# Weight scratch in row layout, six-deep halo rows and kept halo pieces in a hybrid decoder layer

## The reference

```
h2 = rmsnorm(x, g_ffn)
a = relu(h2 @ w_ff1)          # 1024 x 4096
x = x + (a * a) @ w_ff2       # 4096 x 1024
return rmsnorm(x, g_final)
```

## Time and profile before

| | us |
|---|---|
| median of 3 runs | 1951.0 (1950.24 to 1951.74) |
| the profiled execution: its time | 1958.57 |
| its span (slowest core, 0) | 1956.5 |
| spans of the other cores | 1927.8 to 1946.8 |
| PE busy | 1636.5 |
| DVE, ACT busy | 992.8, 756.4 |

### The profile page before, as it was taken

How to read it: one execution, slowest core, us unless ns; L and a number is a source line. 1 busy time by engine, 2 the same in 40 slices (tenths; PEclk the granted TensorE clock), 3 DMA queues, 4 the chain that set the end, 5 groups by cost and what they waited for, 6 DMA issues and landing times.

```text
span 1956.5 us, 30675 instructions; the slowest of 8 cores (1927.8 to 1956.5 us)
## 1 busy us (share of the span) xinstructions
PE 1636.5 (84%) x10130; PEld 864.0 (44%) x10320; DVE 992.8 (51%) x1613; ACT 756.4 (39%) x1481; POOL 66.4 (3%) x114
## 2 busy tenths in 40 slices
PE   2655526889959998899889997999799979998798
PEld 1322215445524553455435543555355524553343
DVE  2333226556536654575546645565456535654434
ACT  2222028235522554255414551355334532544212
POOL 4000000000000000000000000000100000000000
PEclk9867768999979998999989998999899999999899
DMA  9999998234254334442454326333542354324243
GB/s 201 159 148 138 183 165 157 89 123 162 87 195 155 120 129 166 164 143 107 145 188 147 130 109 204 135 141 123 200 157 98 133 180 141 125 89 187 103 157 123
DMA packets 72632, 283.85 MB, mean 145 GB/s; under 512 B 7712, under 2 KB 30496, under 8 KB 49824
## 3 DMA queue, kind: packets, MB, share of 16 engines
q1 hardware_dynamic: 37440, 211.00, 31.3%
q0 software_dynamic: 35040, 70.88, 18.6%
HBM read 287.53 MB, written 39.85 MB: 167 GB/s over the span
## 4 chain that ended last, share of the span: by engine, by line
PE 67%; DMA 15%; DVE 7%; issue 4%; ACT 4%; SPq 2%; DVEq 0%; POOL 0%; ACTq 0%; another core or an unknown queue 0%; POOLq 0%
PE mm L406 32%; PE mm L808 19%; DMA xa<-xh 5%; PE ob L646 5%; PE sc L618 5%; DMA out<-x 5%; PE mm L751 4%; DMA ring<-wscratch 2%; DMA x<-xh 2%; ACT tmp L364 2%; SPq L115 2%; PE tp L387 1%; DVE x L814 1%; DVE hb L377 1%; DVE QA L510 1%
## 5 line engine op out<-in xcount | busy, mean ns | idle before, releaser
L406 PE MATMUL mm<-h2T,ring 128*128 128x512 bf16 x2053 | 500.3, 386 | 33.1 <-DVE KT L521 17.8
L808 PE MATMUL mm<-ring,aT 128*128 128x512 bf16 x1977 | 479.7, 387 | 5.7 <-DVE aT L796 1.2
L620 ACT ACTIVATE P<-sc 128x512 bf16<-128x512 f32 x487 | 283.5, 595 | 220.8 <-PE sc L618 195.8
L406 PEld LDWEIGHTS mm<-h2T,ring 128*128 128x128 bf16 x2128 | 202.7, 99 | 247.4 <-issue 49.2
L808 PEld LDWEIGHTS mm<-ring,aT 128*128 128x128 bf16 x2048 | 196.0, 99 | 217.9 <-issue 31.0
L796 DVE TENSOR_TENSOR aT<-tmp 128x512 bf16<-128x512 f32 x256 | 177.1, 692 | 205.6 <-ACT tmp L795 204.3
L795 ACT ACTIVATE tmp<-mm 128x512 f32<-128x512 f32 x256 | 152.8, 597 | 323.8 <-PE mm L406 312.9
L814 DVE TENSOR_TENSOR x<-x,mm 128x512 f32<-128x512 f32 x256 | 175.5, 685 | 142.1 <-PE mm L808 135.0
L406 PE MATMUL mm<-hT,ring 128*128 128x512 bf16 x809 | 194.5, 392 | 43.9 <-DMA ring<-wscratch 24.9
L629 DVE TENSOR_TENSOR P<-P,E 128x512 bf16<-128x512 bf16 x448 | 185.7, 421 | 71.9 <-ACT P L620 69.7
L646 PE MATMUL ob<-P,Vd 128*128 128x128 bf16 x1792 | 176.2, 222 | 49.7 <-DVE P L629 49.5
(11 more groups left out here) (75 smaller groups left out, 1187.7 us busy)
## 6 DMA issues: line engine op xcount, KB each, us to landing
ring<-wscratch SPq DMA_DIRECT2D x176, 1024.0 KB, 5.4
wscratch<-w_ff POOLq DMA_DIRECT2D x16, 1024.0 KB, 230.8
out<-x POOLq DMA_DIRECT2D x32, 512.0 KB, 3.8
xa<-xh SPq DMA_DIRECT2D x24, 512.0 KB, 12.4
xa<-xh POOLq DMA_DIRECT2D x24, 512.0 KB, 5.3
x<-xh POOLq DMA_DIRECT2D x24, 512.0 KB, 5.6
Vd<-Vd SPq DMA_DIRECT2D x132, 48.0 KB, 2.3
wscratch<-w_in POOLq DMA_DIRECT2D x4, 1024.0 KB, 84.2
```

Of the source, the lines that this page charges most:

```text
L406: T.op("pe", lambda: nc.tensor.matmul(out_ap, lhsT=l, rhs=r, start=(i == 0), stop=(i == n - 1)), reads=reads, writes=[b_out], mark=(i == n ...
L620: T.op("act", lambda: nc.scalar.activation(out=P_[:], in_=s_, func=AF.Exp, bias=bt.get("bias", 0.0)), reads=[bs_], writes=[bP_])
L808: T.op("pe", lambda: nc.tensor.matmul(m_[:], lhsT=aT[:, fl, tc * 128:(tc + 1) * 128], rhs=pf[:, fl % 4, ch * 512:(ch + 1) * 512], start=(f ...
```

## The change

It has five parts. (1) The scratch keeps the weights' own row layout in four tensors. The conversions are 8: `w_in` whole (rows of 2048), `w_out` and the quarters of `w_ff2` flat (4096 elements at a time), `w_ff1` in halves (2048). A ring load of `w_in`, `w_out` or `w_ff1` is then 1024 runs of 512 bf16; one of `w_ff2` is 128 runs of 8 KB, four consecutive rows to a partition, which `ff1` answers by taking every fourth column of its piece as weights. (2) Row blocks for the halo tiles, the memory tokens and tile 4 are requested six deep, in the two `xa` and four of the `x1` buffers; gains that are first needed later are loaded after stage B of tile 4. (3) Only pieces 1 and 2 are loaded directly; `w_in` is converted next, ahead of the memory weights, and piece 3 is loaded from the scratch when tile 2 starts. (4) The three halo pieces stay in the ring for tile 4, which takes them in the order 3, 1, 2, 0; `ring_skip(3)` sets the ring's requests three pieces ahead of their use for the rest of the program. (5) Five PSUM banks serve projections up to tile 4's stage B, stage A of the next tile is spread over the groups of stage B, and the memory phase moves behind tile 2.

```diff
-    sc = nc.dram_tensor("wscratch", [NPIECES, 128, 4096], BF16).ap()
+    s_in = nc.dram_tensor("s_in", [D, 2048], BF16).ap()
+    s_out = nc.dram_tensor("s_out", [D, D], BF16).ap()
+    s_ff1 = nc.dram_tensor("s_ff1", [D, 4096], BF16).ap()
+    s_ff2 = nc.dram_tensor("s_ff2", [4096, D], BF16).ap()
...
+        def ring_src(idx):
+            if idx >= P_FF2:
+                i = idx - P_FF2
+                return s_ff2[512 * i:512 * i + 512, :].rearrange("(p f) c -> p (f c)", f=4), b_cv[f"ff2_{i // 2}"], 1
+            if idx >= P_FF1:
+                i = idx - P_FF1
+                return s_ff1[:, 512 * i:512 * i + 512].rearrange("(k p) c -> p k c", p=128), b_cv[f"ff1_{i // 4}"], 8
...
+        xpool = [(xa[i], b_xa[i], xa_sem[i]) for i in range(2)] + [(x1[i], b_x1[i], x1_sem[i]) for i in range(1, NX1)]
+        halo_rows = [xh[c * 128:(c + 1) * 128, :] for c in range(4 * NHALO)]
+        halo_rows += [memd[c * 128:(c + 1) * 128, :] for c in range(2)]
+        halo_rows += [xh[c * 128:(c + 1) * 128, :] for c in range(4 * NHALO, 4 * NHALO + 4)]
...
+        halo_issue()
+        T.dma("sp", g_sem, gb_mix[:], gbs[0])
+        halo_issue()
+        T.dma("sp", g_sem, csm_t[:], csm[:, :])
         T.dma("sp", g_sem, cpc_t[:], cpc[:, :, :])
...
+        for _ in range(4):
+            halo_issue()
+        T.dma("sp", gm_sem, x1[0][:], gbs[3], writes=[b_x1[0]])
...
-        for pi, slot in ((1, 1), (2, 2), (3, 0)):
-            direct_piece(ring[slot][:], [b_ring[slot]], halo_sem[slot], w_in, 512 * pi)
+        for pi in (1, 2):
+            direct_piece(ring[pi][:], [b_ring[pi]], halo_sem[pi], w_in, 512 * pi)
+            halo_pieces[pi] = (ring[pi], b_ring[pi])
+        halo_pieces[3] = (ring[0], b_ring[0])
+        conv("in", s_in.rearrange("a (b c) -> (a b) c", b=1), w_in.rearrange("a (b c) -> (a b) c", b=1))
         kvm_sem = dsem("kvmsem")
...
-        for i in (0, 1, 2, 3):
-            conv_k(P_WIN + i, w_in, 512 * i)
...
+        def flat4(a):
+            return a.rearrange("(a b) c -> a (b c)", b=4)
+
+        def conv_rest():
+            conv("out", flat4(s_out), flat4(w_out))
+            for h in range(2):
+                conv(f"ff1_{h}", s_ff1[:, 2048 * h:2048 * h + 2048], w_ff1[:, 2048 * h:2048 * h + 2048])
+                for q in (2 * h, 2 * h + 1):
+                    conv(f"ff2_{q}", flat4(s_ff2[1024 * q:1024 * q + 1024, :]), flat4(w_ff2[1024 * q:1024 * q + 1024, :]))
+
+        def b_order(j):
+            return [3, 1, 2, 0] if j == NHALO else [0, 1, 2, 3]
...
+        def ring_skip(n):
+            rs["issued"] += n
...
-            i = cnt["mm"] % 2
+            i = cnt["mm"] % (5 if wide["on"] else 2)
...
-                c0 = (fl % 4) * 128
-                mm_group(m_[:], bm_, [(pk[:, k, c0:c0 + 128], h2T[:, k, :]) for k in range(8)], [b_piece, b_h2T])
+                mm_group(m_[:], bm_, [(pk[:, k, fl % 4::4], h2T[:, k, :]) for k in range(8)], [b_piece, b_h2T])
...
+        wide["on"] = True
+        ring_skip(3)
         for c in range(4):
             stage_A_chunk(0, c)
...
+                stage_B(j, gh)
+                wide["on"] = False
+                if j == NHALO:
+                    T.dma("sp", gf_sem, gb_ffn[:], gbs[1])
+                    T.dma("sp", gf_sem, gb_fin[:], gbs[2])
...
-                    stage_A_begin(nxt)
-                    stage_A_elem(nxt, 0)
-                    stage_A_elem(nxt, 1)
-                    hooks = [lambda: (stage_A_pe(nxt, 0), stage_A_elem(nxt, 2)),
-                             lambda: (stage_A_pe(nxt, 1), stage_A_elem(nxt, 3))]
+                bg, en, pe_ = stage_A_begin_elem, stage_A_end_elem, stage_A_pe
+                gh = {0: lambda: bg(nxt, 0), 1: lambda: (en(nxt, 0), bg(nxt, 1)), 2: lambda: pe_(nxt, 0),
+                      3: lambda: (en(nxt, 1), bg(nxt, 2)), 4: lambda: pe_(nxt, 1),
+                      5: lambda: (en(nxt, 2), bg(nxt, 3)), 6: lambda: pe_(nxt, 2), 7: lambda: en(nxt, 3)}
+                if j == 2:
+                    T.dma("sp", ring_sem[0], ring[0][:].rearrange("p (k c) -> p k c", k=8), ring_src(P_WIN + 3)[0],
+                          reads=[b_cv["in"]], writes=[b_ring[0]])
...
-                if j == 1:
+                if j == 2:
                     mem_phase()
```

More of the change, by code:

```diff
@@ L243, in build_nc, with conv @@
         b_tp = Buf("tp")
[L245 to L252, removed]
+        b_cv = {k: Buf(k) for k in ("in", "out", "ff1_0", "ff1_1", "ff2_0", "ff2_1", "ff2_2", "ff2_3")}
+        cv_sem = {k: dsem("cv" + k) for k in b_cv}
+        def conv(key, dst, src):
+            T.dma("pool", cv_sem[key], dst, src, writes=[b_cv[key]])
+        def ring_src(idx):
[5 more added lines that the diff above has]
+                return s_ff1[:, 512 * i:512 * i + 512].rearrange("(k p) c -> p k c", p=128), b_cv[f"ff1_{i // 4}"], 8
+            if idx >= P_WOUT:
+                i = idx - P_WOUT
+                return s_out[:, 512 * i:512 * i + 512].rearrange("(k p) c -> p k c", p=128), b_cv["out"], 8
+            i = idx - P_WIN
+            return s_in[:, 512 * i:512 * i + 512].rearrange("(k p) c -> p k c", p=128), b_cv["in"], 8
         hv_col = csm_t[:, 0:1]
@@ L276, in load_xa @@
             r0 = j * TOK + c * 128
-            return load_xa_rows(xh[r0:r0 + 128, :], x_queue(j))
+            e = x_queue(j)
+            s_ = xa_state["n"] % 2
+            xa_state["n"] += 1
+            T.dma(e, (xa_sem if e == "sp" else xa_psem)[s_], xa[s_][:], xh[r0:r0 + 128, :], writes=[b_xa[s_]])
+            return xa[s_], b_xa[s_]
         a_slots = {}
@@ L311, in build_nc @@
         b_c.w = tot
-        for i in (0, 1, 2, 3):
-            conv_k(P_WIN + i, w_in, 512 * i)
[L314 to L322, removed]
+        def flat4(a):
[6 more added lines that the diff above has]
+                    conv(f"ff2_{q}", flat4(s_ff2[1024 * q:1024 * q + 1024, :]), flat4(w_ff2[1024 * q:1024 * q + 1024, :]))
+        conv_rest()
+        def b_order(j):
+            return [3, 1, 2, 0] if j == NHALO else [0, 1, 2, 3]
         seq = []
@@ L329, in build_nc @@
         for j in range(NHALO, NT):
-            seq += [P_WIN + 0, P_WIN + 1, P_WIN + 2, P_WIN + 3]
+            seq += [P_WIN + i for i in b_order(j)]
             if j > NHALO:
@@ L343, in ring_issue @@
             idx = seq[n]
-            T.dma("sp", ring_sem[s], ring[s][:], sc[idx], reads=[b_sc_piece[idx]], writes=[b_ring[s]])
+            src, b_src, k = ring_src(idx)
+            dst = ring[s][:].rearrange("p (k c) -> p k c", k=k) if k > 1 else ring[s][:]
+            T.dma("sp", ring_sem[s], dst, src, reads=[b_src], writes=[b_ring[s]])
             rs["issued"] = n + 1
@@ L378, in rms_end @@
                                                                op0=ALU.mult, op1=ALU.mult),
-                 reads=[b_src, bs, b_g] + list(extra_reads), writes=[b_dst])
+                 reads=[b_src, bs, b_gain] + list(extra_reads), writes=[b_dst])
             return hbs[hi], b_dst
@@ L776, in stage_L_end @@
                                                                op0=ALU.mult, op1=ALU.mult),
-                 reads=[bs, b_g], writes=[bx])
+                 reads=[bs, b_gf], writes=[bx])
             T.dma("pool", osem, ov[tc], xt[:], reads=[bx])
```

82 lines of the change are left out of this document (41 added, 41 removed).

## The result

The changed kernel takes 1991.4 us (median; 1989.2 in its profiled execution) against 1951.1 us: ratio 1.0204, interval 1.0184 to 1.0224, so 40 us slower. The forecast was 1971 us, slower. All medians and ratios here are of the executions in which neither half of the chip ran at a lower clock than the other.

The account below looks back on a forecast made before the run. The first 340 us were taken as bound by DMA, the later part by TensorE. Tile 5's rows +29, small gains -14, costs +1 and +4 give +20 us: 1971 us, own range 1930 to 2010, with rivals 1860 to 2010.

Parts of the forecast that it names:

- Turns, one packet each: DMA engines, both queues full: one packet of each queue in turn, whatever its size; q1 needs 608 packets, q0 488.
- DRAM traffic of some 330 GB/s whatever the packets: First 340 us: DRAM traffic stays near 330 GB/s with short and long packets; 96 MB take 291 us.
- Rival B: Conversions gain from long runs and end at 225 to 240 us; 1926 us in all; chance 11%.
- The size of a conversion packet: Conversions on q0: w_in and w_ff1 write packets of 4 KB, w_out and the w_ff2 quarters 8 KB.
- Start of tile 4, 165 to 180 us: End of the halo: stage B of tile 4 starts then against 213.23 us, 33 to 48 us gained.
- Piece 0, 32 to 42 us: Tile 4's stage B: piece 0 needs 64 turns with w_ff1 packets, 32 to 42 us; stage B ends at 235 to 270.
- The end of the conversions, 275 us: Conversions end at 275 us (226 to 291 computed), so tile 5's rows land at 312 us, +29 us.
- 283.4 us: Landing time of tile 5's first rows in the kernel before, against which the forecast 312 us gave +29 us.
- The range, 1930 to 2010 us: Whole kernel: the forecast's own range around 1971 us, most of it 1950 to 2000.
- Three requests ahead, -14, and costs of +5: Behind tile 5's rows: earlier ring requests save 14 us; strided weights cost +1, slower ring pieces +4.
- rival C: All tiles: 1 KB ring runs fall behind; a piece landing in 12 us adds 52 us, 2020 us; chance 10%.
- Rival A: Start of the kernel: q1 isn't starved, tile 5's rows land at 190 us; 1848 us, or 1895; chance 25%.

Follow-up runs that it names:

- e1_small: Changed kernel with every conversion cut into columns of 512, so that it writes 1 KB runs; 1 KB ring runs kept: 1929.5 us, ratio 0.988 to the kernel before.
- e7_ff2long: Kernel before with only w_ff2 converted into rows in one run (long packets) and ff1's weights taken with stride 4: 1988.9 us, ratio 1.020.
- e2_pad: Changed kernel with padded scratch rows, so conversions of w_in, w_out and w_ff2 write 4, 2 and 8 KB packets: 1985.4 us, ratio 1.016 to the kernel before.
- e3_old: Changed kernel with the old scratch, its 22 conversions, ring loads and unstrided ff1 weights, new schedule kept: 1900.6 us, ratio 0.973 to the kernel before.
- e5_xafirst: As e3_old, with tile 5's first rows requested ahead of gains, V copies and residual rows, and tile 6's rows on SP: 1888.3 us, ratio 0.969.
- e9_afterorder: Changed kernel with tile 5's first rows requested ahead of gains, V copies and residual rows, and tile 6's on SP: 1992.9 us, ratio 1.019 to the kernel before.

## Why the prediction was right, and where its sizes were off

The direction, the place and the mechanism were as forecast; the sizes were not, and the loss was twice the forecast one.

- *Turns, one packet each.* Right: wherever both queues are full the counts are equal or nearly so, from 1 KB against 1 KB to 33 KB against 4 KB, and even in 2 us (7 to 7 at 290 us). That the turns cost the time is shown by e1_small (only q0's packets changed, -60 us) and by e7_ff2long (q0's packets lengthened on the kernel before, +39 us). The Trainium skill (DMA: Bandwidth & Descriptors, Queues, rings and completion order) has 9 to 17 descriptors to a turn; in these runs each recorded packet was a turn of its own, 1 KB runs too.
- *DRAM traffic of some 330 GB/s whatever the packets.* Right: 298 to 358 GB/s. Rival B is out, since the conversions ended at 297 us and not at 225 to 240. Per KB written, a 33 KB packet took 139 ns, a 4.1 KB packet 120 (0.49 us, and not the 0.39 of my bound), a 1 KB packet 172, or 133 in e1_small at 230 us: long packets gained nothing clear.
- *The size of a conversion packet.* Wrong: I took 4 and 8 KB, rows as written in the code. `w_in`, `w_out` and `w_ff2` had 33 KB: a copy that is contiguous on both sides was no longer cut by rows, and padded rows brought the cuts back. e2_pad prices this error at 5 to 9 us (1991.4 against 1985.4; by the ratios 0.0045), hardly more than the intervals leave open.
- *Start of tile 4, 165 to 180 us.* It was 193.3; PE stood 38.4 us in tile 3 while ACT waited for row blocks beside long packets (tile 4 starts at 145.3 us in e2_pad, earlier than I forecast).
- *Piece 0, 32 to 42 us.* PE stood 74.5 us for it, and stage B of tile 4 ended at 300 us, outside the 235 to 270 that I gave.
- *The end of the conversions, 275 us.* It was 293 to 297. This is the term that was mis-sized: I had worked out 291 us from the traffic and then took 275, as a compromise with a bound (0.39 us per 4 KB packet) for which no row spoke. With 291 + 3 + 34 the rows land at 328 us; they landed at 327.6. That is +44 and not +29, and the whole forecast is then 1986 us. The close hit is in part luck, for the way there was another: piece 0 landed at 291.4, stage B took 8.5 us more, SP then needed 16.6 us to come to `xa`, and the rows took 11. And the 283.4 us that I subtracted belong to the latest of the eight cores before; their mean is 274.3, so the rows came 51 us later and not 44.
- *The range, 1930 to 2010 us.* Its own terms add up to 1912 (1951 - 25 - 14) and 2016 (1951 + 57 - 14 + 22). The result lies in either. And DMA stood at 9 in six slices before, not seven; its share of 1.00 up to 340 us is right.
- *Three requests ahead, -14, and costs of +5.* Behind the first output projection -12.8 was measured on the slowest cores and -10.1 in the mean of all, expected was -9. PE's ring waits behind 350 us (against the earlier trace rows):

```profile
PE mm L798 <- DMA ring<-s_out: 10.8, 1, 10.8
...
PE mm L854 <- DMA ring<-s_ff: 1.7, 1, 1.7
```

19.0 us went to 10.8 and the 6.2 us in `ff1` are gone; 1.7 in `ff2` is new. A ring piece with 1 KB runs lands in 6.2 to 6.4 us and not 5.4; rival C did not happen. The strided `ff1` weights (page, columns of its part 5):

```profile
L455 PEld LDWEIGHTS mm<-h2T,ring 128*128 128x128 bf16 x2088 | 225.7, 113 | 186.3 <-issue 13.3
```

They take 113 ns against 98, and in e7_ff2long, which has them too, nothing behind the first output projection got longer.

- *Rival A* was the likeliest way to be wrong. e3_old is the nearest to what it stood for: 1901 us when q1 is not starved, where I had put 1848 to 1895.

## What to carry to other kernels

In all windows here in which both DMA queues were full, the engines dealt out their bandwidth by packets, not by bytes: a background copy with long runs starved a foreground one with short runs (33 KB against 4 KB, 14 GB/s for the foreground). Before lengthening the runs of a background transfer, count the packets that each queue has to move up to the next thing that is waited for; if the foreground has more, it ends with the background. Cut such background copies short on purpose (-60 us in e1_small), and look at what stands in front of the request that is waited for. Moving it up helps only where nothing slow is left in front of it, and it must not put another one back (e5_xafirst, e9_afterorder).

## What the hardware showed that I had not expected

A copy whose source and destination are contiguous went out in packets of 33 KB written, 4.6 us each, although its access pattern named rows of 4 KB; padding each row by 64 elements was enough to get rows again. A queue of short runs alone is not slow: 1426 packets of 1 KB in 5 us, 288 GB/s. And SP can be held in a single request, with no wait that the profile shows: 68.65 us in the changed kernel, 35.67 us for one gain in e2_pad.
